# Attention in a two-layer hybrid generator: scores issued as pairs of heads, four probability buffers, value halves alternating

## What is computed

```python
def gqa_attend(qg, k, v):
    s = jnp.einsum('bqkgd,bskd->bkgqs', qg, k).astype(jnp.float32) * (HEAD_DIM ** -0.5)
    p = jax.nn.softmax(s, axis=-1).astype(v.dtype)
    return jnp.einsum('bkgqs,bskd->bqkgd', p, v)
```

## Time and profile before

| | |
|---|---|
| median of 3 runs | 2337.09 us (2336.42 to 2337.12) |
| profiled execution, its own time | 2338.05 us |
| its span | 2336.3 us |
| mean granted TensorE clock | 0.977 of full |
| busy time in the span: PE, DVE, ACT | 2217.6, 1727.9, 1132.2 us (95, 74, 48%) |
| attention of layer 0 | from 169.15 to 233.55 us |
| attention of layer 1 | from 1032.07 to 1076.34 us |

### The profile page before, as it was taken

One profiled execution on the slowest core, in us unless ns is written; L12 is line 12 of the kernel. 1 busy time (PEld: TensorE's weight loads), 2 busy tenths in 40 slices (PEclk: granted clock), 3 DMA queues, 4 the chain that ended last, 5 costly groups with the idle time before them and its releaser, 6 DMA issues.

```text
span 2336.3 us, 33202 instructions
## 1 busy us (share of the span) xinstructions
PE 2217.6 (95%) x12554; PEld 1868.1 (80%) x12554; DVE 1727.9 (74%) x2384; ACT 1132.2 (48%) x1502; POOL 42.7 (2%) x84
## 2 busy tenths in 40 slices
PE   7989999997999999789997999999999999999998
PEld 6754776655777777657986999999999999999997
DVE  6776587646666766776736888888888888888886
ACT  3315221213333232434324766767676666767675
POOL 0000000000000000000000000000000000000000
PEclk9998999999999999889997999999999999999999
DMA  7500144343444443312535898989898998989895
GB/s 302 183 30 1 68 155 161 127 144 119 160 152 162 144 144 126 116 43 78 183 123 215 318 355 306 361 303 359 311 353 325 337 359 303 361 303 358 311 348 194
DMA packets 61296, 513.89 MB, mean 220 GB/s; under 512 B 6963, under 2 KB 8115, under 8 KB 21045
## 3 DMA queue, kind: packets, MB, share of 16 engines
q1 hardware_dynamic: 49716, 471.16, 54.0%
q0 software_dynamic: 11520, 41.95, 5.0%
HBM read 512.03 MB, written 1.05 MB: 220 GB/s over the span
## 4 chain that ended last, share of the span: by engine, by line
PE 87%; DVE 7%; ACT 2%; issue 2%; DMA 1%; SPq 0%; DVEq 0%; ACTq 0%
PE bank L752 9%; PE bank L754 9%; PE bank L753 9%; PE bank L505 5%; PE bank L506 5%; PE bank L507 5%; PE bank L617 5%; PE bank L768 4%; PE bank L769 4%; PE bank L770 4%; PE bank L627 4%; PE bank L461 2%; PE bank L673 2%; PE bank L659 2%; PE bank L649 2%
## 5 line engine op out<-in xcount | busy, mean ns | idle before, releaser
L1448 DVE TENSOR_TENSOR m_low<-W,m_high 128x2048 fp32r<-128x2048 f32 x225 | 515.7, 2292 | 126.1 <-ACT m_high L1000 126.1
L752 PE MATMUL bank<-m_high,gathered_high 128*128 128x256 f32 x1792 | 508.7, 284 | 13.8 <-DVE m_low L1448 12.4
L754 PE MATMUL bank<-m_low,gathered_high 128*128 128x256 f32 x1792 | 507.7, 283 | 0.0
L753 PE MATMUL bank<-m_high,gathered_low 128*128 128x256 f32 x1792 | 507.0, 283 | 0.0
L1000 ACT ACTIVATE m_high<-W 128x2048 fp32r<-128x2048 f32 x225 | 431.9, 1920 | 8.2 <-issue 7.9
L752 PEld LDWEIGHTS bank<-m_high,gathered_high 128*128 128x128 f32 x1792 | 342.7, 191 | 25.2 <-DVE m_low L1448 14.8
L753 PEld LDWEIGHTS bank<-m_high,gathered_low 128*128 128x128 f32 x1792 | 342.7, 191 | 8.0
L754 PEld LDWEIGHTS bank<-m_low,gathered_high 128*128 128x128 f32 x1792 | 342.7, 191 | 0.0
L1451 DVE TENSOR_TENSOR m_low<-W,m_high 128x1024 fp32r<-128x1024 f32 x225 | 274.4, 1219 | 0.0
L505 PE MATMUL bank<-h_high,tile_high 128*128 128x512 f32 (+1 forms) x704 | 259.1, 368 | 11.7 <-DVE tile_low L1178 11.7
L1002 ACT ACTIVATE m_high<-W 128x1024 fp32r<-128x1024 f32 x225 | 237.2, 1054 | 6.8 <-PE bank L770 6.8
(11 more groups left out here) (216 smaller groups left out, 3559.2 us busy)
## 6 DMA issues: line engine op xcount, KB each, us to landing
W<-in_moe SPq DMA_DIRECT2D x225, 1536.0 KB, 8.3
W<-in_w_mod_later POOLq DMA_DIRECT2D x80, 512.0 KB, 3.6
W<-in_ffn SPq DMA_DIRECT2D x33, 1024.0 KB, 4.8
W<-in_attn_blocks SPq DMA_DIRECT2D x24, 1280.0 KB, 5.8
W<-in_attn_blocks SPq DMA_DIRECT2D x22, 1024.0 KB, 5.1
W<-in_attn_blocks SPq DMA_DIRECT2D x8, 1536.0 KB, 6.9
shift_tiles<-in_w_mod_first SPq DMA_DIRECT2D x8, 512.0 KB, 14.0
scale_tiles<-in_w_mod_first SPq DMA_DIRECT2D x8, 512.0 KB, 14.8
```

Source lines behind the costliest of these rows:

```text
L752: mm(b[:, 0:256], hgh[:, k, :], m13h[:, u % 2, k, :], start=k == 0, stop=False)
L753: mm(b[:, 0:256], hgl[:, k, :], m13h[:, u % 2, k, :], start=False, stop=False)
L754: last = mm(b[:, 0:256], hgh[:, k, :], m13l[:, u % 2, k, :], start=False, stop=k == KD - 1)
L1448: tt(m13l[:, u % 2], chunk[u][:, 0:2 * D].rearrange("p (k n) -> p k n", k=KD), m13h[:, u % 2].bitcast(F32), ALU.subtract).then_inc(S("moe_ ...
```

## The change

TensorE's order is now in turns p of two units: S(2p), S(2p+1), T(2p-3), T(2p-2), and V((p-3)/2) in every odd turn from the third on. `psum_order` follows it. The middle of the stretch reads S6 S7 T3 T4 V0, S8 S9 T5 T6, S10 S11 T7 T8 V1. The two scores of a turn are of an even and an odd head, on different halves of the partitions. ScalarE's order for an odd u is K(u-4), E(u), K(u-3), for an even u E(u) alone: K3 stands between E6 and E7. The probability buffers are four, the fourth being `root`. In `values` the chunk is the outer loop and the half the inner one, so instructions for the two halves alternate. C(v) of VectorE keeps its place: it comes after M(4v+8) and N(4v+7).

```diff
--- before.py
+++ after.py
@@ -76,8 +76,6 @@
 LOGITS, EQUAL, FIRST, REST, SECOND, MASK, COMB, RANK, TOP, GAP, ODDS, WEIGHT = range(12)
 
 
-LAG = 3
-
 
 def attention_units(layer):
 
@@ -96,13 +94,11 @@
     order += [f"f{s}{c}" for s in streams for c in range(2)] + [f"p{s}{c}" for s in streams for c in range(2)]
     order += ["dup0", "dup1"]
     n = len(attention_units(layer))
-    for u in range(n + LAG + 1):
-        if u < n:
-            order.append(f"S{u}")
-        if LAG <= u < n + LAG:
-            order.append(f"T{u - LAG}")
-        if u > LAG and (u - LAG - 1) % 4 == 3:
-            order.append(f"V{(u - LAG - 1) // 4}")
+    for p in range(n // 2 + 2):
+        order += [f"S{u}" for u in (2 * p, 2 * p + 1) if u < n]
+        order += [f"T{u}" for u in (2 * p - 3, 2 * p - 2) if 0 <= u < n]
+        if p >= 3 and p % 2:
+            order.append(f"V{(p - 3) // 2}")
     for i in BRANCH_ORDER:
         if i == 1:
             order.append("convnorm")
@@ -216,6 +212,7 @@
         Xp = at("Xp", [2, T], attnT_at + 2 * T)
         ht = at("ht", [4, LAT], attnT_at)
         nsq = sg
+        probs = [prob[:, 0], prob[:, 1], prob[:, 2], root]
 
         top[0] = shared
         shift0 = at("shift_tiles", [KD, D])
@@ -466,7 +463,7 @@
                     nxt("prob_ready")
                     b = opened(layer, f"T{u}")
                     for c in range(4 - 2 * s):
-                        last = pe.transpose(b[:, c * P:(c + 1) * P], prob[:, u % 3, c * P:(c + 1) * P], C("ident"))
+                        last = pe.transpose(b[:, c * P:(c + 1) * P], probs[u % 4][:, c * P:(c + 1) * P], C("ident"))
                     done(layer, f"T{u}", last)
 
                 def values(v):
@@ -475,19 +472,22 @@
                         read(pe, layer, f"T{u}")
                     b = opened(layer, f"V{v}")
                     n = 4 - 2 * s
-                    for half in range(2):
-                        for c in range(n):
+                    for c in range(n):
+                        for half in range(2):
                             last = mm(b[64 * half:64 * half + 64, 0:256], vtok[:, 2 * s + c, 64 * g:64 * g + 64],
                                       pT[:, v % 2, c, half::2, :], start=c == 0, stop=c == n - 1)
                     done(layer, f"V{v}", last)
 
-                for u in range(len(units) + LAG + 1):
-                    if u < len(units):
-                        scores(u)
-                    if LAG <= u < len(units) + LAG:
-                        turned(u - LAG)
-                    if u > LAG and (u - LAG - 1) % 4 == 3:
-                        values((u - LAG - 1) // 4)
+                n = len(units)
+                for p in range(n // 2 + 2):
+                    if 2 * p < n:
+                        scores(2 * p)
+                        scores(2 * p + 1)
+                    for u in (2 * p - 3, 2 * p - 2):
+                        if 0 <= u < n:
+                            turned(u)
+                    if p >= 3 and p % 2:
+                        values((p - 3) // 2)
 
             def attention_half(layer):
                 N = T if layer == 0 else LAT
@@ -927,15 +927,17 @@
                     fn(pT[:, v % 2, 0:n, j, :], b[:, 0:n * P].rearrange("p (c q) -> p c q", q=P), ACT.Copy) \
                         .then_inc(free(layer, f"T{u}"), 1)
 
-                for u in range(len(units) + LAG):
-                    if u >= LAG:
-                        keep_turned(u - LAG)
+                for u in range(len(units) + 4):
+                    if u % 2 and u >= 4:
+                        keep_turned(u - 4)
                     if u < len(units):
                         n = T if units[u][0] == 0 else CTX
                         nxt("negmax_ready")
                         b = filled(act, layer, f"S{u}")
-                        fn(prob[:, u % 3, 0:n], b[:, 0:n], ACT.Exp, bias=stat[:, u % 4, 0:1], scale=HD ** -0.5,
+                        fn(probs[u % 4][:, 0:n], b[:, 0:n], ACT.Exp, bias=stat[:, u % 4, 0:1], scale=HD ** -0.5,
                            accum_out=stat[:, u % 4, 1:2]).then_inc(free(layer, f"S{u}"), 1)
+                    if u % 2 and 3 <= u < len(units) + 3:
+                        keep_turned(u - 3)
 
                 step = 0
                 for i in BRANCH_ORDER:
@@ -1264,7 +1266,7 @@
                     n = T if units[u][0] == 0 else CTX
                     read(dve, layer, f"S{u}")
                     step(dve.reciprocal(stat[:, u % 4, 2:3], stat[:, u % 4, 1:2]))
-                    ts(prob[:, u % 3, 0:n], prob[:, u % 3, 0:n], stat[:, u % 4, 2:3], None, ALU.mult) \
+                    ts(probs[u % 4][:, 0:n], probs[u % 4][:, 0:n], stat[:, u % 4, 2:3], None, ALU.mult) \
                         .then_inc(S("prob_ready"), 1)
 
                 def keep_values(v):
@@ -1274,13 +1276,13 @@
                     dve.tensor_copy(attnT[:, 2 * g:2 * g + 2, q0:q0 + P], b[:, 0:256].rearrange("p (c q) -> p c q", q=P)) \
                         .then_inc(free(layer, f"V{v}"), 1)
 
-                for u in range(len(units) + LAG + 2):
+                for u in range(len(units) + 5):
                     if u < len(units):
                         maximum(u)
                     if 1 <= u <= len(units):
                         normalise(u - 1)
-                    if u > LAG + 1 and (u - LAG - 2) % 4 == 3:
-                        keep_values((u - LAG - 2) // 4)
+                    if u >= 8 and u % 4 == 0:
+                        keep_values((u - 8) // 4)
 
 
                 dve.wait_ge(S("conv_gated"), 2 * layer + 2)
```

## The result

The changed kernel takes **2326.32 us**, the median of 5 runs (2324.66 to 2327.68), against 2337.09 before. The ratio is 0.9954, with a 95% interval of 0.9941 to 0.9966: 10.8 us or 0.46% faster. The profiled execution has a span of 2325.9 us against 2336.3.

What follows compares the result with a forecast made beforehand. TensorE bounds the kernel now; next, value blocks wait for ScalarE's copy. Profiled 2338.05 us less 11.7 (8.8 + 2.0 + 2.5 - 1.6) is 2326.35; with the median 0.96 lower, 2325.4, rounded to 2325.5; range 2320.7 to 2333.0.

Steps and rivals of the forecast that it cites:

- The total: Forecast time of the whole changed kernel: 2325.5 us.
- the range: 2320.7 to 2333.0 us for the whole kernel, taking the forecast with its bounds and rival 2.
- the sign: The whole kernel faster by over 0.2%, below 2332.4 us; chance 0.83.
- TensorE's gain: In attention, a score pair takes about 1.1 us, a latent value block 1.9 instead of 2.79; context block saves nothing.
- rival 2: Alternating halves in value blocks overlap no better than now; latent block stays at 2.79 us, total 2332.6; chance 0.12.
- The loop: Value block waits for ScalarE's copy behind an exponential; latent group 8.6 us against 9.35, 0.8 saved.
- rival 1: TensorE's own 6.5 us set the latent group, the loop being softer; 25.2 us saved, total 2312; chance 0.03.
- The context groups: Context attention groups take 5.8 us against 5.00, 0.8 lost in each; 1.6 lost over four groups.
- The start: Start of each layer's attention: first value block begins 4.0 us earlier and takes 3.2; 4.4 us saved per layer.
- up to 1.8 more per layer: Bound on the attention starts: extra us saved if the clock returns before the first value block.
- the sum: Starts 8.8, layer 0 2.0 and layer 1 2.5 us saved, context 1.6 lost: 11.7 us saved.
- Rival 3: TensorE's clock does not come back, with waits before every value block; 11.0 us slower, total 2348; chance 0.08.

Runs made afterwards that it cites:

- copy_first: The changed kernel with ScalarE's order as before the change, the copy of T(u-3) ahead of exponential u; 2309.54 us, ratio 0.9884.
- values_late: The changed kernel with each value block one turn later on TensorE and its copy one unit later on VectorE; 2307.79 us, ratio 0.9873.
- pairs_only: The changed kernel with the value block's loops as before, one half then the other; 2334.30 us, ratio 0.9990.
- fill_values: The changed kernel with one extra, overwritten 512-column matmul at the head of every value block, before its waits; 2319.61 us, ratio 0.9929.
- fill_start_before: The kernel before with two extra, overwritten 512-column matmuls ahead of T0's wait at each attention start; 2321.84 us, ratio 0.9943.
- values_only: The kernel before with only the value block's two loops exchanged, so that halves alternate; 2330.36 us, ratio 0.9973.

## Why the prediction was right, and where it was not

**The total.** 2325.5 was put, 2326.32 measured; the range and the sign hold. Part of that nearness is luck, as the terms below show.

**TensorE's gain.** Right in both terms: a pair 1.06 against 1.1, a latent block 1.88 against 1.9, a context block unchanged, 1.01 (213.33 to 214.34). That halves alternate in one bank was the open point of rival 2; it falls.

**The loop.** Right. 8.56 against 8.6 us for a latent group, 5.77 against 5.8 for a context one; the wait before the value block is 1.63 us where "about 1" was put, and another 0.60 stands ahead of T8, for VectorE's scaling. copy_first and values_late, which only move the copy or the block, show that the wait bounds the group. The gain of 25 us that rival 1 worked out from TensorE's own time is about what values_late reaches (29.6): only the loop, with the low clock that its waits brought, stood between the change and that.

**The context groups.** 0.8 lost in each, as put (5.77 against 5.00).

**The start.** This step was mis-sized: 4.4 us a layer were put. S8 starts 13.74 us after S0 (182.85 less 169.11) against 20.29 (189.44 less 169.15), 6.5 saved, and in layer 1 13.96 against 20.28, 6.3 saved. The failed clause is that the clock comes back only with V0. It came back at about 177.5, after one pair of scores, both halves of the array streaming, and eight transposes. So V0 took 1.88 us where 3.2 was put, and it started 7.84 us after T0 where 8.5 was put, in spite of a wait of 1.44 for T3's copy where 0.3 was put. The new value loops don't bring the clock back: in pairs_only, with the old ones, S6 and S7 take 1.06 us at 177.82. Whether the pairs do, or the eight transposes in a row that come with the new order, no run separates. The upper bound of the step, "up to 1.8 more per layer", was passed, by 2.1 and 1.9. The low spell that is left costs next to nothing: in fill_values' layer 1, where the clock stayed at 1.00, V0 comes 11.7 us after S0, in its layer 0, with the spell, 11.8.

**The clock later.** Missing from the sum. The waits that the loop makes cost clock: V2 1.6 us in layer 0 and 1.7 in layer 1, the end of layer 0's attention about 2 (V6 0.5, V7 0.9, the transposes between the rest, against fill_values, where the clock is at 1.00), and 0.7 in the first gate projection (nine matmuls in 2.88 us instead of 2.19). Rival 3 had the mechanism, that the clock falls where TensorE waits, but not its measure: short spells, not the whole stretch. fill_values, which fills these waits, takes 5.8 us off, about 1 of it not the clock's. So two errors of the sum, 4 too little at the starts and 6 too little at the waits, nearly cancel: 11.7 + 4 - 6 = 9.7, where 10.4 were measured in the span. The 0.7 between lie in part between the layers, where 0.4 was gained in spite of the gate projection's loss.

**Rival 3 and the transposes.** The page TensorE: Matmul & The Clock Gate of the Trainium skill has transposes not count as activity the way matmuls do (Part 4: PE-mode transpose). Here fill_start_before runs scores on half the array and transposes by turns, without a wait, and keeps 1.00, and so does values_only's layer 1; in the kernel before the same sequence, entered at 0.50, did not raise it in 11 us. The runs don't separate transposes from half-array scores, so what they count as stays open.

**What stays open.** When the clock falls at a wait and when not. Behind waits that are alike it fell at V2 in both layers of the changed kernel, at V1, V2 and V3 of layer 0 and at no value block of layer 1 in pairs_only, and at V4 and V5, in the context groups, in neither. At the start of attention, behind the same wait of 2.03 to 2.04 us, it fell in 14 of the 16 stretches of the eight profiled executions that don't fill it and not in the other two (layer 1 of values_only and of fill_values); in all four stretches with the wait filled it stayed at 1.00. No run changes only when a wait comes.

## What to carry to other kernels

When an engine stops being the bound, write out the loop from one wait of its stream to the next, through the **order** of the other engines' streams; here a copy behind one exponential took 17 us, low clock included, more than the change brought. Judge each edit by itself: two exchanged loops alone were worth 6 to 7 of 10.8 us, the pairs with their order 2 to 3, the fourth buffer nothing. And ask for each new wait of TensorE what the clock does with it; work that is thrown away can be cheaper than a wait, but only where TensorE is the bound at all.

## What the runs showed of the hardware

- How far matmuls on different halves of the array ran side by side depended on how near they stand in the stream: eight after eight took 2.79 us, alternating 1.88; four after four took 1.02, alternating 1.01.
- Behind a wait of 2.04 us with nothing running the granted clock was at half within 1 us in layer 0 of the kernel before, and stayed so through more than 11 us of gapless single scores and transposes. Behind the same wait it fell in 14 of 16 profiled stretches; with 2 us of throwaway matmuls in it, it stayed at 1.00 in four of four, worth 6.3 us a layer in the old order and nothing in the order of values_late. In the new order, with score pairs, it was back at 177.5.
- With waits of about 1.6 us every 8.6 the clock fell at some value blocks and not at others; in the profiled execution with 1.0 us of each filled it fell at none.
- TensorE resumed 0.25 us after the copy it waited for, where its instruction stood behind five semaphore waits, 0.14 behind three in fill_values, and 0.05 after VectorE's scaling, behind one (187.20 to 187.25, at T8).
